# Half 1 of the input requested later in a hybrid trunk kernel, its squares and its mean moved into the work on half 0

## The reference

```
mod = (silu(c) @ ada_w[l] + ada_b[l])          # six vectors of 1024: shift, scale, gate, twice
h = rmsnorm(x, norm_g[l, 0]) * (1 + sc1) + sh1  # rmsnorm: x * rsqrt(mean(x*x) + eps) * g
y = even_mixer(h, ...)                          # first step: h @ w_in, then attention
```

## Time and profile before

| what | value |
|---|---|
| median of 3 runs | 2658.5 us (2657.66 to 2662.53) |
| time of the profiled execution | 2661.66 us |
| its span, first to last instruction | 2659.7 us |
| TensorE busy | 2523.3 us, 95% of the span |
| mean granted TensorE clock | 0.986 of full |
| start of the first `xn` of half 0 | 46.56 us |
| start of the first `xn` of half 1 | 61.10 us |
| first transposes of the attention | 92.89 us |

### The profile page before, as it was taken

One profiled execution on the slowest core, in us unless ns is written; L12 is line 12 of the kernel. 1 busy time (PEld: TensorE's weight loads), 2 busy tenths in 40 slices (PEclk: granted clock), 3 DMA queues, 4 the chain that ended last, 5 costly groups with the idle time before them and its releaser, 6 DMA issues.

```text
span 2659.7 us, 33905 instructions
## 1 busy us (share of the span) xinstructions
PE 2523.3 (95%) x12152; PEld 2063.6 (78%) x12152; DVE 1360.0 (51%) x1877; ACT 1078.4 (41%) x1837; POOL 1150.2 (43%) x648
## 2 busy tenths in 40 slices
PE   5999999998999999999999999998999999999996
PEld 3777777777778888888887778887878888888885
DVE  6576665542465333555356536668466332355145
ACT  3354544343454332335233326656554333334222
POOL 0111111011656777444444434444656777544443
PEclk8999999999999999999999999999999999999998
DMA  6233332324333122443434741223233222343343
GB/s 265 65 110 103 112 102 84 98 92 174 95 108 107 66 94 79 135 143 95 160 125 163 274 141 64 71 71 127 88 99 115 80 87 72 117 144 111 111 135 110
DMA packets 106886, 305.14 MB, mean 115 GB/s; under 512 B 11456, under 2 KB 11776, under 8 KB 106752
## 3 DMA queue, kind: packets, MB, share of 16 engines
q1 hardware_dynamic: 106752, 303.40, 33.9%
HBM read 262.46 MB, written 40.89 MB: 114 GB/s over the span
## 4 chain that ended last, share of the span: by engine, by line
PE 61%; issue 17%; POOL 7%; DVE 6%; ACT 3%; DVEq 2%; DMA 2%; POOLq 2%; SPq 1%; ACTq 0%
PE ps L826 8%; PE ps L830 8%; PE ps L827 8%; PE ps L1225 5%; PE ps L1226 5%; POOL w_lo L700 5%; PE ps L1229 5%; PE ps L988 3%; PE ps L1256 3%; PE ps L1259 3%; PE ps L1253 3%; PE ps L1057 2%; PE ps L954 2%; PE ps L975 2%; DVEq L2262 1%
## 5 line engine op out<-in xcount | busy, mean ns | idle before, releaser
L700 POOL TENSOR_TENSOR w_lo<-w_raw,w_hi 128x1024 fp32r<-128x1024 f32 x258 | 634.5, 2462 | 1316.6 <-ACT w_hi L1324 571.0
L826 PE MATMUL ps<-h_hi,w_hi 128*128 128x512 f32 x1272 | 510.2, 401 | 17.6 <-DVE h_lo L1866 7.3
L827 PE MATMUL ps<-h_lo,w_hi 128*128 128x512 f32 x1272 | 499.2, 392 | 0.0
L1324 ACT ACTIVATE w_hi<-w_raw 128x1024 fp32r<-128x1024 f32 x178 | 188.3, 1059 | 437.5 <-PE ps L1259 288.7
L830 PE MATMUL ps<-h_hi,w_lo 128*128 128x512 f32 x1272 | 315.5, 390 | 0.0
L1934 DVE TENSOR_TENSOR a_lo<-arena,a_hi 128x512 fp32r<-128x512 f32 x88 | 205.5, 2336 | 208.2 <-ACT a_hi L1791 208.2
L826 PEld LDWEIGHTS ps<-h_hi,w_hi 128*128 128x128 f32 x1272 | 240.7, 189 | 83.6 <-DVE h_lo L1866 14.4
L827 PEld LDWEIGHTS ps<-h_lo,w_hi 128*128 128x128 f32 x1272 | 241.1, 190 | 50.3 <-issue 2.4
L830 PEld LDWEIGHTS ps<-h_hi,w_lo 128*128 128x128 f32 x1272 | 239.8, 189 | 50.1
L1225 PE MATMUL ps<-comb,w_hi 128*128 128x512 f32 x560 | 217.8, 389 | 0.0
L1226 PE MATMUL ps<-comb,w_hi 128*128 128x512 f32 x560 | 217.8, 389 | 0.0
(11 more groups left out here) (269 smaller groups left out, 4255.7 us busy)
## 6 DMA issues: line engine op xcount, KB each, us to landing
w_raw<-weights SPq DMA_DIRECT2D x286, 512.0 KB, 3.6
arena<-ada_w SPq DMA_DIRECT2D x80, 512.0 KB, 3.6
arena<-act_d SPq DMA_DIRECT2D x72, 256.0 KB, 3.7
act_d<-ybuf SPq DMA_DIRECT2D x56, 256.0 KB, 2.2
arena<-ada_w SPq DMA_DIRECT2D x8, 1024.0 KB, 14.9
x<-xT SPq DMA_DIRECT2D x4, 2048.0 KB, 13.3
glr<-weights SPq DMA_DIRECT2D x14, 512.0 KB, 3.6
rinv<-weights SPq DMA_DIRECT2D x28, 256.0 KB, 4.1
```

Source lines behind the costliest of these rows:

```text
L700: pool.tensor_tensor(w_lo[:, s, :], w_raw[:, s, :], w_hi[:, s, :].bitcast(f32), ALU.subtract).then_inc(lo_done, 1)
L826: pe.matmul(bank(b), w, high[:, k, :], start=k == 0, stop=False)
L827: pe.matmul(bank(b), w, low[:, k, :], start=False, stop=False)
L1324: a.activation(w_hi[:, slot, :], w_raw[:, slot, :], ACT.Copy).then_inc(hi_done, 1)
```

## The change

Half 1 of x is requested behind all modulation pieces and the first two weight units, in SyncE's list just before the wait for `mod_done`. Half 1's squares become four instructions of 128x1024, one behind each `write_h(k)` of half 0 for `k` = 1 to 4; only every second one raises `sq_first`. TensorE no longer does half 1's mean around the group-1 matmuls: its two parts stand inside chunk 0, before the products of `k` = 4 and `k` = 6. ScalarE's root for half 1 moves from behind `k` = 2 to behind `k` = 7 of half 0.

```diff
 # SyncE
-                    if (g, u) in ((0, 4), (1, 4)):
-                        sp.dma_start(x[:, :, g * HALF:(g + 1) * HALF], x_in[:, :, g * HALF:(g + 1) * HALF]).then_inc(s_x[g], 16)
+                    if (g, u) == (0, 4):
+                        sp.dma_start(x[:, :, 0:HALF], x_in[:, :, 0:HALF]).then_inc(s_x[0], 16)
...
             def attention():
                 raw(0)
                 raw(1)
+                sp.dma_start(x[:, :, HALF:S], x_in[:, :, HALF:S]).then_inc(s_x[1], 16)
                 sp.wait_ge(mod_done, 1)
 # TensorE
+                    if parts and k in (4, 6):
+                        mean(0, 0, 1, k // 2 - 2)
...
-                unit(u, u % 2, chunk_bank(c), half if c in (0, 2) else None, hh[half], hl[half], done=ch_done)
+                unit(u, u % 2, chunk_bank(c), half if c in (0, 2) else None, hh[half], hl[half], done=ch_done, parts=c == 0)
...
                 if g:
-                    mean(0, 0, 1, 0)
                     pe.wait_ge(acc_done, 1)
...
             mm.then_inc(ada_mm, 1)
-            mean(0, 0, 1, 1)
 # ScalarE
-                op.then_inc(sq_first, 1)
+                if (k0 + n) % 4 == 0:
+                    op.then_inc(sq_first, 1)
...
             root(0, 0, 0)
-            first_square(1, 0, 4)
-            first_square(1, 4, 4)
             hi_u(0)
             hi_u(1)
             a.wait_ge(mod_done, 1)
             for half in range(2):
                 for k in range(KB):
                     write_h(k, None, -1, (0, 0, half))
-                    if half == 0 and k == 2:
+                    if half == 0 and 0 < k < 5:
+                        first_square(1, 2 * k - 2, 2)
+                    if half == 0 and k == KB - 1:
                         root(0, 0, 1)
```

More of the change, by code:

```diff
@@ L811, in _, with unit @@
             pe.sem_inc(pv_done, 1)
-            def unit(use, s, b, job=None, high=h_hi, low=h_lo, y_new=False, done=unit_used, mid=None):
+            def unit(use, s, b, job=None, high=h_hi, low=h_lo, y_new=False, done=unit_used, mid=None, parts=False):
                 pe.wait_ge(hi_done, use + 1)
```

## The result

The changed kernel takes 2669.34 us (median of 7 runs, 2664.34 to 2677.06), the kernel before 2659.89 us beside it (7 runs, 2657.66 to 2662.53). The ratio is 1.0042, with a 95% interval of 1.003 to 1.0054: slower, by 8 to 14 us. The forecast was 2669.7 us, +11.2. The profiled execution took 2668.10 us.

What follows compares the result with a forecast made beforehand. It took TensorE, busy 95% of the span, as the bound, delayed by T and the distance from T to half 1's first `xn`. Terms +1.5 + 8.2 + 1.5 = +11.2 on 2658.5 gave 2669.7 us, range 2663 to 2676.

Steps and rivals of the forecast that it cites:

- The weights' `w_lo` collide with the multiply-adds: GpSimd and VectorE take turns during group 1's multiply-adds: sum 2.2 us later, while the gain gets 2.0 us shorter.
- Group 1's records at the low clock: TensorE, idle before the 16 group-1 matmuls, runs them at clock 0.50: +1.3 us, bounds 0 and +1.3.
- T: Start of half 0's first `xn`, 46.56 us before: forecast 48.1, +1.5, bounds -3.9 and +4.1.
- ScalarE's squares: Half 1's squares among half 0's high parts: low part of `k` = 4 at T + 7.9, of `k` = 7 at T + 12.0.
- The mean inside chunk 0: Half 1's mean on TensorE delays half 1's first `xn` from T + 14.5 to T + 22.7: +8.2 us, bounds +5.4 and +13.
- Chunk 2's clock: TensorE, fed one pair each 1.33 us in chunk 2, may fall to half clock: +1.5 us, ends 0 and 3.4.
- The sum: Total of the terms for the whole kernel: +1.5 + 8.2 + 1.5 = +11.2 us, median 2669.7.
- (c): Multiply-adds on VectorE not held by `w_lo`, ending at 39.98, T moving -2.6: 2665.6 us; chance 0.1.
- (a): Half 1's mean in chunk 0 costs the small price, at full clock from its start: 2662 to 2665 us; chance 0.17.
- (b): Low clock through both parts of the mean, falling again in chunk 2: 2673 to 2676 us; chance 0.1.
- (d): Faster: the mean hidden in chunk 0's gaps on TensorE, only T counting: 2654.6 to 2655.9 us; chance 0.03.
- (e): No difference that can be told, a later wait taking up the shift: some 2658.5 us; chance 0.05.

Runs made afterwards that it cites:

- e2: Changed kernel with GpSimd waiting for the group-1 sum before its first `w_lo`; 2665.74 us, ratio to the kernel before 1.0028.
- e5: Changed kernel with 15 extra 512-column matmuls on TensorE between the group-0 and group-1 records; 2667.61 us, ratio to the kernel before 1.0027.
- r2: The changed kernel timed and profiled again, nothing altered; 2669.37 us, ratio to the kernel before 1.003.
- e1: Changed kernel with SyncE's old request order restored, so only half 1's squares, mean and root are moved; 2666.26 us, ratio to the kernel before 1.0023.
- e3: Changed kernel, late request kept, with half 1's squares behind the weight copies and its whole mean ahead of chunk 0; 2663.2 us, ratio to the kernel before 1.0009.
- r1: The kernel before, profiled again with nothing altered; 2660.49 us.
- e8: The kernel of e7 with half 1 requested ahead of the two weight units and its squares split; 2657.46 us, ratio to the kernel before 0.9982.
- e4: The kernel before with only GpSimd's second `w_lo` moved behind half 0's h; 2659.28 us, ratio 0.9998.
- e6: Changed kernel with e3's and e4's edits and the first `w_lo` behind the group-1 sum; 2658.23 us, ratio to the kernel before 0.9991.
- e7: The kernel of e6 with ten extra 512-column matmuls between the group-0 and group-1 records; 2659.29 us, ratio to the kernel before 0.9994.

## Why the prediction was right

By its own steps:

- **The weights' `w_lo` collide with the multiply-adds.** Right in mechanism and size: the second and third took 3.45 and 3.20 us, the sum ended at 44.64 (forecast 44.1; the reciprocal ahead of it had started 0.5 us later than before), and e2 took the collision away. The gain fell by 2.04 (forecast 2.0).
- **Group 1's records at the low clock.** Right, somewhat larger: 3.59 against 1.80, +1.8, outside the bound of +1.3. The forecast took the 15 records that a window of 2.90 us touches for 15 that fit in it. A record in that stream lasts 0.35 us (mean of 29 in the trace of before, 1577 to 1582.7) and overlaps the next, so they start (2.90 + 0.35) / 15 = 0.217 us apart, and 16 take 15 x 0.217 + 0.35 = 3.6. e5 shows that it was the clock.
- **T.** +2.3 (48.89), +2.0 in r2; forecast +1.5. The sum ended 2.75 later, but the records had waited before for the mean until 42.14 and not for the sum at 41.89, so they started 2.6 later; the forecast counted from the sum, 0.25 too much.
- **ScalarE's squares.** Their cost is less than forecast: the low part of `k` = 4 ended at T + 7.7, as before, and the last one at T + 11.5, not T + 12.0.
- **The mean inside chunk 0.** Right in place and kind, e1 and e3 show it from both sides. Its size was 7.2 us (H1 - T of 21.73 against 14.54), 7.8 in r2; forecast 8.2. The first part took 5.43 and 6.03 against 6.2.
- **Chunk 2's clock.** The forecast 1.5 us did not come, and its ground was wrong too: it had TensorE at the pace of a pair each 1.33 us for some 8 us. TensorE's timeline of the changed kernel, at chunk 2's first and fifth pair:

```profile
76.28 0.50 PE L829 MATMUL ps<-h_hi,w_hi 128*128 128x512 f32 x1 [1.66 <-DVE qk_flat L2084]
...
78.92 0.50 PE L829 MATMUL ps<-h_hi,w_hi 128*128 128x512 f32 x1 [0.52 <-DVE h_lo L1868]
```

Chunk 2 waits for VectorE's first eviction (L2084) until 76.28. By then three pairs are ready and the fourth is in time, so these four run back to back, and only the last four, 78.92 to 82.84, come some 1.3 us apart. That is the same number as in the kernel before (69.41 to 73.32). The windows show the clock up throughout:

```profile
76.30:82.80 6.50, 4.31 (x14) 2.29 (x14) 6.48 (x10) 3.37 (x5) 0.00 (x0) 1.00 0.00 0
82.80:85.20 2.40, 2.36 (x10) 1.99 (x11) 0.00 (x0) 0.00 (x0) 0.00 (x0) 1.00 0.00 0
```

The fall comes in some executions, in the kernel before too (r1), so it should have been a width and not a term.

- **The sum.** 2.3 + 7.2 + 0 = 9.5 at the transposes, and 9.45 us between the medians. The forecast 11.2 was 1.7 too high, nearly all of it the term of chunk 2's clock; the mean's 1.0 too much was made good by T's 0.8 too little. The agreement of 2669.34 with 2669.7 is closer than that by luck: the median of before beside it was 2659.89 and not the 2658.5 on which the sum stood. That 9.5 at the transposes meets 9.45 between the medians is in part chance too, since the stages behind move by several us (r1).
- **Rivals.** (c) is out by the multiply-adds; (a) by the mean's first part, which was slow, and (b) by its second, which ran at the full clock; (d) and (e) by H1 and A. What is left open: why e8's time is further below before than its stages, and why the changed kernel's runs spread over 13 us and those of before over 5 to 10 (31 of them beside e1 to e4 went from 2655.37 to 2665.10).

## What to carry to other kernels

Work that an idle engine does ahead of the path is free where it stands; moving it to make a transfer earlier puts it on the path unless its new place is idle and its consumer asks late enough (7.0 us in e1, nothing at H1 - T in e3). Before a transfer is moved up, follow who is released by it: here the earlier weights woke GpSimd in the middle of VectorE's chain and cost more (4.1 us on the multiply-adds) than the earlier piece gave (they began 1.3 us earlier) and the gain that was freed (2.0). And TensorE, emptied of the work that it did while it waited, was at the low clock when its 16 critical records came: 3.59 us instead of 1.80.

## What the runs showed that I had not expected

Ten extra matmuls whose results nobody uses brought T 1.6 us forward (44.24 in e6, 42.63 in e7), and all of it was gone at H1 (58.80 and 58.83), because half 1's squares held ScalarE. Two profiles of one kernel can differ by 2 us at the same mark of the first 100 us (92.89 and 94.95), and by 3.9 us in a stage that is the same, so the moments of one profile were compared only up to the transposes.
